# The first mixer's recurrence over blocks of 128 tokens instead of chunks of 64, with a second, further decayed copy of half the queries

## What is computed

```
def _gla_scan(q, k, v, log_a, s0):        # CHUNK = 64
    def step(s, inp):
        qc, kc, vc, gc = inp
        b = jnp.cumsum(gc, axis=2)
        b_last = b[:, :, -1:, :]
        q_dec = qc * jnp.exp(b)
        scores = jnp.einsum('bhld,bhmd->bhlm', q_dec, kc * jnp.exp(-b))
        scores = jnp.where(mask, scores, 0.0)
        o = (jnp.einsum('bhlm,bhmv->bhlv', scores, vc)
             + jnp.einsum('bhld,bhdv->bhlv', q_dec, s))
        s_new = (jnp.exp(b_last[:, :, 0, :, None]) * s
                 + jnp.einsum('bhld,bhlv->bhdv', kc * jnp.exp(b_last - b), vc))
        return s_new, o
```

## Time and profile before

| | us |
|---|---|
| three runs | 2849.07, 2850.6, 2851.8 |
| median | 2850.6 |
| span of the profiled execution | 2836.0 |
| PE busy in that span | 2684.6 (95%) |
| DVE busy | 1397.8 (49%) |
| ACT busy | 1005.6 (35%) |
| the eight GLA scans | 1636 to 1936 |

### The profile page before, as it was taken

How to read it: one execution, slowest core, us unless ns; L and a number is a source line. 1 busy time by engine, 2 the same in 40 slices (tenths; PEclk the granted TensorE clock), 3 DMA queues, 4 the chain that set the end, 5 groups by cost and what they waited for, 6 DMA issues and landing times.

```text
span 2836.0 us, 36376 instructions
## 1 busy us (share of the span) xinstructions
PE 2684.6 (95%) x14292; PEld 2183.0 (77%) x14292; DVE 1397.8 (49%) x1833; ACT 1005.6 (35%) x1694; POOL 818.7 (29%) x645
## 2 busy tenths in 40 slices
PE   7988999999999889999999899998999899999998
PEld 6966788888798667888887676666877688788887
DVE  2748755543327586554433445546445534433332
ACT  5458622222244695222222444353223200222222
POOL 5566623343236465244343010031001011100000
PEclk9999999999999999999999899998999999999999
DMA  6230034554422100355454111111112133233232
GB/s 134 84 62 1 11 88 134 150 140 125 132 85 82 49 1 27 90 141 152 131 141 132 33 49 45 42 33 45 45 32 59 30 104 116 74 93 104 80 92 81
DMA packets 396730, 230.46 MB, mean 81 GB/s; under 512 B 9772, under 2 KB 392876, under 8 KB 396560
## 3 DMA queue, kind: packets, MB, share of 16 engines
q1 hardware_dynamic: 394608, 226.19, 28.7%
q0 software_dynamic: 1952, 1.94, 0.9%
HBM read 226.01 MB, written 2.10 MB: 80 GB/s over the span
## 4 chain that ended last, share of the span: by engine, by line
PE 77%; DVE 9%; ACT 7%; DMA 5%; issue 2%; SPq 0%; POOL 0%; DVEq 0%; ACTq 0%; POOLq 0%
PE ps L842 65%; PE scores L842 8%; DMA raws<-in_w_down 4%; PE ps L987 1%; ACT wH L1841 1%; DVE R L2193 1%; DVE wL L2403 1%; DMA ring<-in_w_in 1%; DVE ring_parts L2456 1%; DVE spare L2203 0%; ACT U L1680 0%; DVE R L2521 0%; DVE QK_parts L2183 0%; ACT spare L1703 0%; ACT R L1708 0%
## 5 line engine op out<-in xcount | busy, mean ns | idle before, releaser
L842 PE MATMUL ps<-xH,wH 128*128 128x512 f32 x1000 | 395.0, 395 | 6.5 <-DVE xL L2378 4.1
L842 PE MATMUL ps<-xL,wH 128*128 128x512 f32 x1000 | 390.7, 391 | 0.0
L842 PE MATMUL ps<-xH,wL 128*128 128x512 f32 x1000 | 390.0, 390 | 0.0
L1841 ACT ACTIVATE wH<-raws 128x2048 fp32r<-128x2048 f32 (+1 forms) x114 | 193.0, 1693 | 495.2 <-PE ps L842 356.6
L842 PE MATMUL ps<-ring_parts,U_parts 128*128 128x256 f32 (+2 forms) x2000 | 337.8, 296 | 18.8 <-DVE ring_parts L2260 6.2
L2403 DVE TENSOR_TENSOR wL<-raws,wH 128x2048 fp32r<-128x2048 f32 (+1 forms) x114 | 231.7, 2032 | 247.3 <-ACT wH L1841 246.0
L842 PEld LDWEIGHTS ps<-ring_parts,U_parts 128*128 128x128 f32 x2000 | 295.3, 201 | 35.1 <-issue 30.4
L842 PE MATMUL ps<-R 128*64 128x128 f32 (+3 forms) x1688 | 242.1, 334 | 30.7 <-DVE R_parts L2214 7.0
L808 POOL CAST ring_parts<-ring 128x2048 fp32r<-128x2048 f32 x34 | 67.0, 1969 | 648.9 <-DMA ring<-in_w_in 573.5
L733 POOL TENSOR_TENSOR spare<-spare,cvec 128x1024 f32<-128x1024 f32 x64 | 122.8, 1919 | 441.3 <-DMA spare<-in_w_ada 441.3
L842 PEld LDWEIGHTS ps<-R 128*64 128x64 f32 (+2 forms) x1688 | 157.3, 166 | 112.1 <-issue 61.8
(11 more groups left out here) (444 smaller groups left out, 4762.5 us busy)
## 6 DMA issues: line engine op xcount, KB each, us to landing
raws<-in_w_gate_up SPq DMA_DIRECT2D x88, 512.0 KB, 5.6
ring<-in_w_in SPq DMA_DIRECT2D x34, 1024.0 KB, 5.7
spare<-in_w_ada SPq DMA_DIRECT2D x64, 512.0 KB, 3.9
raws<-in_w_down SPq DMA_DIRECT2D x32, 704.0 KB, 6.0
raws<-in_w_ffn_in SPq DMA_DIRECT2D x44, 512.0 KB, 5.1
ring<-in_w_in SPq DMA_DIRECT2D x26, 512.0 KB, 5.4
raws<-in_w_ffn_out SPq DMA_DIRECT2D x16, 704.0 KB, 4.6
ring<-in_w_o SPq DMA_DIRECT2D x12, 448.0 KB, 3.7
```

The costliest lines, as they stand in the source:

```text
L842: return nc.tensor.matmul(o, a, b, start=first, stop=last)
L1841: ap.do(f(wH[:, g % 2, 0:n], raws[:, g % 2, 0:n], ACT.Copy), wh_ready)
```

## The change

The GLA recurrence goes over 6 blocks of 128 tokens instead of 12 chunks of 64. The sums of the decay logarithms still run inside 64-token chunks, so the query and key factors stay as they are. What crosses from one chunk of a block to the other is put together from their parts:

- `ends` holds for each chunk what the state decays by up to the block's end; its two small operations stand in `decay_sums` ahead of the subtraction that gives the keys' factor.
- `qd` has three groups of 64 queries for each tile: the first chunk's, the second chunk's, and the second chunk's scaled by the decay through the first. `decayed` makes that copy with one more multiplication, and the decay of a block (`block_decay`) with another small one. The wait for ACT's `dec` moves from ahead of `masked` into `decayed`.
- The scores matmul takes all three groups (192 columns), so four tiles need two banks. `masked` makes two copies for each bank.
- There are 5 state jobs of 128 rows instead of 11 of 64, with six filler matmuls behind each, and 4 DVE steps of the recurrence behind the first copy instead of 10.
- An output job is two matmuls of 128 x 128 weights instead of one such and two of 128 x 64.
- The table `tri` grows from 256 to 384 columns. `ST` and `qd` lie in the memory that `ST` had.

```diff
-                bank = db.fill(pe)
-                for j in range(TT):
-                    ins = mm(bank[:, j * P:(j + 1) * P], ki[:, d, j * P:(j + 1) * P], qd[:, d, j * P:(j + 1) * P], True, True)
-                ins.then_inc(d_full, 1)
+                for pair in range(2):
+                    bank = db.fill(pe)
+                    for n in range(2):
+                        j = 2 * pair + n
+                        ins = mm(bank[:, n * 3 * CH:(n + 1) * 3 * CH], ki[:, d, j * P:(j + 1) * P],
+                                 qd[:, d, j].rearrange("p g c -> p (g c)"), True, True)
+                    ins.then_inc(d_full, 1)
...
-                order = gla_order(d)[:-1]
-                for c in order:
-                    b_, t = c % 2 * CH, c // 2
-                    job(db, lambda b: b[:, 0:DV], [(kdt[b_:b_ + CH, t, :], v_[b_:b_ + CH, t, 0:DV])])
-                    if order.index(c) % 2:
-                        some(beside_states, 2)
+                for t in block_order(d)[:-1]:
+                    job(db, lambda b: b[:, 0:DV], [(kdt[:, t, :], v_[:, t, 0:DV])])
+                    some(beside_states, 2)
...
                 for j in range(TT):
-                    bank = db.fill(pe)
-                    mm(bank[:, 0:DV], SC[:, d, j, :], v_[:, CT + j, 0:DV], True, False)
-                    for half in range(2):
-                        s_ = gla_order(d).index(4 + 2 * j + half)
-                        ins = mm(bank[half * CH:(half + 1) * CH, 0:DV], qd[:, d, j * P + half * CH:j * P + (half + 1) * CH],
-                                 ST[:, s_, 0:DV], False, True)
-                    ins.then_inc(d_full, 1)
+                    s_ = block_order(d).index(CT + j)
+                    job(db, lambda b: b[:, 0:DV], [(SC[:, d, j, :], v_[:, CT + j, 0:DV]),
+                                                   (block_queries(d, j), ST[:, s_, 0:DV])])
...
-                vp.do(v.tensor_tensor(W1.rearrange("p (c l) -> p c l", l=CH), bc(last, CH, 2), b, ALU.subtract), b2_ready)
+                vp.do(v.tensor_copy(ends[:, :], last))
+                vp.do(v.tensor_tensor(ends[:, d::2], last[:, d::2], last[:, 1 - d::2], ALU.add))
+                vp.do(v.tensor_tensor(W1.rearrange("p (c l) -> p c l", l=CH), bc(ends[:, :], CH, 2), b, ALU.subtract), b2_ready)
...
+                vp.more(dec_ready)
+                vp.do(v.tensor_tensor(block_decay[:, d, :], dec[:, d, 0::2], dec[:, d, 1::2], ALU.mult))
+                through = dec[:, d, 4 + d::2]
+                vp.do(v.tensor_tensor(qd[:, d, :, 2 - 2 * d, :], qd[:, d, :, 2 * d, :], bc(through, CH, 2), ALU.mult))
...
             def masked(d):
-                bank = db.take(dve)
-                vp.do(v.copy_predicated(SC[:, d], bc(tri[:, d, :], TT, 1), bank[:, :].rearrange("p (a c) -> p a c", a=TT)), d_free)
+                for pair in range(2):
+                    bank = db.take(dve)
+                    x = bank[:, 0:2 * 3 * CH].rearrange("p (a c) -> p a c", a=2)
+                    into = SC[:, d, 2 * pair:2 * pair + 2, :]
+                    at_, last = (1 - d) * CH, 2 * d * CH
+                    vp.do(v.copy_predicated(into, bc(tri[:, d, 0:P], 2, 1), x[:, :, at_:at_ + P]))
+                    vp.do(v.copy_predicated(into[:, :, (1 - d) * CH:(2 - d) * CH], bc(tri[:, d, P:P + CH], 2, 1), x[:, :, last:last + CH]), d_free)
                 vp.also(sc_ready)
```

More of the change, by code:

```diff
@@ L130, in build @@
         wup = C[0:2 * RANK, 1536:2560].rearrange("p (a b) -> p a b", a=2)
+        ends = sb("ends", [P, NC2])
+        block_decay = sb("block_decay", [P, 2, NC2 // 2])
         rt = sb("rt", [P, TT])
@@ L2538, in _ @@
             for h in range(NH2):
-                vp.more(dec_ready)
                 masked(0)
@@ L2546, in _ @@
                     second_low("v", h + 1)
-                states(gla_order(0), ST, DV, lambda c: dec[:, 0, c:c + 1])
+                states(block_order(0), ST, DV, lambda c: block_decay[:, 0, c:c + 1])
                 decay_sums(h, 1)
@@ L2554, in _ @@
                 gla_outputs(0)
-                vp.more(dec_ready)
                 masked(1)
-                states(gla_order(1), ST, DV, lambda c: dec[:, 1, c:c + 1])
+                states(block_order(1), ST, DV, lambda c: block_decay[:, 1, c:c + 1])
                 if h + 1 < NH2:
@@ L2656, in mlstm_outputs @@
                     y_subtract(KT - 1, KT)
-                states(mlstm_order(d), STm, DV + 1, lambda c: dec[:, d, c:c + 1])
+                states(block_order(d), STm, DV + 1, lambda c: dec[:, d, c:c + 1])
                 for t in range(TT):
```

26 lines of the change are left out of this document (15 added, 11 removed).

## The result

| | before | after |
|---|---|---|
| median of four runs each, us | 2851.2 | 2819.5 |
| lowest and highest | 2849.07, 2853.16 | 2812.45, 2823.27 |
| span of the profiled execution | 2836.0 | 2810.6 |
| GLA stage: first state copy on DVE to the end of the last output | 288.2 | 257.3 |

The ratio is 0.9895, with a 95% interval from 0.9875 to 0.9915. The forecast was 2819.6. The median fell by 31.7 us, where 31 were forecast. The stage in the last row runs from 1647.70 to 1935.85 before and from 1642.41 to 1899.73 after. It is 30.8 us shorter. The span is only 25.4 us shorter: what lies ahead of the stage took 5.3 us less and what lies behind it 10.7 us more, both in unchanged code. The changed kernel was run and profiled a second time, and there the stage took 261.0 us. The later sections come back to both.

A forecast was written before the change was run, and what follows sets the result against it. PE was taken to bound the GLA scans. 22.8 - 1.9 + 11.2 - 2.1 - 0.7 + 1.3 = 30.6, taken as 31 because the last outputs ran at half clock: 2850.6 - 31 = 2819.6 us, range 2811 to 2832.

The forecast's parts named there:

- State jobs: GLA recurrence on PE: 0.43 us a job against 0.82 to 0.84 a pair; 3.2 us a scan, 22.8 in all.
- Outputs: Output jobs on PE: 0.86 us instead of 1.21, so 0.35 for each of 32 jobs, 11.2 us gained.
- Scores: Scores matmuls on PE: 64 more columns cost 0.43 us for four tiles, paid in five scans, -2.1 us.
- Masks: DVE's masked copies: 1.6 us, about 1 more; hidden except in head 3, direction 0, charged -0.7 us.
- The weights' low halves: PE's three direction 1 waits for DVE's weight subtraction: 0.4 us gained each, +1.3, leaving about 0.3 each.
- Head 3, direction 0: No state gain in this scan: PE waits about 3.6 us more for ACT's permuting copies; clock charged -1.9.
- its charge for the clock: Head 3, direction 0: a second PE gap may bring 3.9 us at half clock, -1.9 us, bounds 0 and -3.5.
- The distance of 14.6 us: Gap between the profiled execution's span, 2836.0 us, and the median of runs, 2850.6, kept unchanged in the forecast.
- the shape is not the price: Rival on state and output jobs: a 128-row job costs 0.84 us like a pair; gain 10, 2840 us; chance 0.07.
- concurrency is all: Rival: a pair of state jobs or output halves costs one matmul, nothing more; 2850 us, no change; chance 0.03.
- another engine catching up: Rival: DVE slack, second scores bank, masks and last-head contention cost 3 + 2 + 4; gain 22, 2829 us; chance 0.12.
- The slower one: Rival: PE's clock at 0.50 more often, GLA stretch mean clock 0.87, time 2857 us; chance 0.03.

The follow-up runs named there:

- the shape alone: The kernel before with all 11 state jobs kept but each contracting 128 rows instead of 64; one run took 2847.9 us.
- the count alone: The kernel before with 5 state jobs for each scan, still of 64 rows, and the matching DVE steps left out; one run took 2840.0 us.
- the outputs alone: The kernel before with only the output jobs changed, to two matmuls of 128 x 128 weights instead of three matmuls; 2836.9 us, ratio 0.9971.
- the states alone: The kernel before with only 5 state jobs of 128 rows and 4 recurrence steps; decays, scores and outputs as they were; 2822.0 us, ratio 0.9922.
- Narrow scores: The changed kernel with the scores undone: four matmuls of 128 columns in one bank, one masked copy of 512 elements; one run took 2805.3 us.
- the low half earlier: The changed kernel with the low-half subtraction for the second mixer's first values moved ahead of head 2, direction 1's outputs; 2809.3 us, ratio 0.9874.
- both edits: The changed kernel with that low-half subtraction moved earlier and POOL permuting six feature tiles instead of five; 2808.9 us, ratio 0.9864.
- a second edit: The changed kernel with six feature tiles permuted by POOL and two by ACT, instead of five and three; 2814.7 us, ratio 0.9891.

## Why the prediction was right

**State jobs: right, both sizes.** Forecast was 0.43 us a job and 3.2 a scan. Measured are 0.42 with fillers of 256 columns and 0.45 with 512. The states of head 1, direction 0, took 10.84 us before and take 1714.87 - 1707.59 + 0.43 = 7.71 now, which is 3.1 less. The experiments show the reason too: at a place in the list neither the shape alone nor the count alone gives anything.

**Outputs: right for the job, with a cost behind them that was not charged.** 0.35 us for each of 32 jobs, by the changed kernel and by the outputs alone. But from the last output of head 0 to the transposes of its norm it takes 5.57 us instead of 4.58, and in head 1 5.33 instead of 4.49. DVE's four scalings there now run beside POOL's cast of the next weights, and take 2.60 us instead of 1.60:

```profile
1711.45 1.60 DVE L2521 TENSOR_SCALAR R<-R,rsg 128x256 f32<-128x256 f32 x4
```

```profile
1696.34 1.89 POOL L811 CAST ring_parts<-ring 128x2048 fp32r<-128x2048 f32 x1 [9.38 <-DMA ring<-in_w_in]
1696.95 2.60 DVE L2533 TENSOR_SCALAR R<-R,rsg 128x256 f32<-128x256 f32 x4
1699.66 1.97 PE L1371 MATMUL ps<-ident,R 128*128 128x128 f32 x8 [1.16 <-DVEq L56]
```

The longer waits appear with the outputs alone (1.44 and 0.80 us) and not with the states alone.

**Scores: too low.** 0.43 was charged for a scan, and narrowing them gives 0.58 back. Over the five scans in which they count that is 0.8 us more than the 2.1 of the sum, within the bound.

**Masks: right in size (1.5 us for 1.6), and right in price where it was charged.** Narrow scores give 0.68 us back from head 2's last output to the transposes in head 3, where 0.7 was charged. Against the kernel before it shows as only 0.08 us (8.11 for 8.03), since the subtraction that queues behind the masks took 2.45 us instead of 2.83.

**The weights' low halves: right, a little better.** Before, 0.73 us each. Forecast were 0.3 us each, and measured 0.22. PE's waits for them in the stage:

```profile
PE ps L845 <- DVE ring_parts L2455: 0.4, 2, 0.2
```

**Head 3, direction 0: the mechanism was right, the sum of it by luck.** PE waits 2.92 us for the permuted tokens instead of a forecast 3.6 (3.97 in the second profile of the changed kernel, 3.8 with the states alone). The scan gains 0.65 us in the first profile instead of nothing and loses 3.07 in the second. The stretch at half clock behind the wait, which was charged with 1.9 us, did not come in the first profile; in the second the clock is 0.50 from 1855 to 1861. These are PE's stretches at that wait (us, PE busy, granted clock, DMA share, GB/s), and ahead of them one between head 0 and head 1, for which nothing had been charged:

```profile
1700.00:1704.00 4.00, 4.00 (x17) 0.64 0.02 4
...
1844.00:1848.00 4.00, 1.11 (x8) 1.00 0.00 0
1848.00:1852.00 4.00, 3.96 (x33) 1.00 0.01 2
```

The first row and the longer wait just ahead of it (1.16 us instead of 0.16) are why head 0 to head 1 took 14.21 us instead of 11.90. So a fall of the clock was charged, and one came, but at another place. From head 1 to head 2 it was the other way round: the clock fell there before and not in the first profile after, which is the 0.93 us that this piece got shorter. Nor was the place in the prediction a fixed one: with the low half earlier the clock was 0.50 from 1852 to 1856, right behind a wait of 4.66 us.

**The sum.** By the pieces of the table, the six scans of heads 0 to 2 give 3.44 + 3.30 + 3.30 + 3.92 + 3.89 + 3.95 = 21.8 us, head 3 gives 0.65 and 2.27, and the pieces between give back 3.4 (3 x 0.25 + 2.31 - 0.93 + 0.64 + 0.59 = 3.36). The outputs give 6 x 1.05 in heads 0 to 2 and 1.38 and 1.84 in head 3, 9.5 together. That is all of the stage's 30.8 us, where 31 were forecast. That the first profile comes so near is partly luck: by the second the stage is 27.2 us shorter. The two differ by the clock. An estimate from the granted clock of slices of 2 us: if each slice is shortened by the share that its clock lacks to 1.00, the stage is 279.6 us before and 247.1 and 247.3 in the two profiles after. That is a gain of 32.3 to 32.5, and the forecast without its charge for the clock is 32.5.

**The distance of 14.6 us was a misreading without effect.** The prediction kept 14.6 us between span and median as if it lay around the span. In the run of the changed kernel that was profiled, the time was 2812.45 and the span 2810.6. So only 1.85 us lie around the span. If the same holds before, its profiled execution took about 2838 us, the fastest of its kernel on record (2838.04 to 2858.4 in later sessions). Since the sum was a difference, nothing hung on it.

**Rivals.** That the shape is not the price would have left state jobs of 0.84 and 2840 us, and the new timeline has 0.42 to 0.45. That concurrency is all needed pairs of 0.43, and the earlier trace rows already had 0.82. The third, another engine catching up, came true in parts: 0.15 us for the second bank, the wait in head 3, and 0.8 to 1.0 us in each of heads 1 and 2 for DVE beside POOL. DVE's slack in direction 1 held, by 0.32 us in head 0 and by almost nothing in head 1. The slower one needed a mean clock of 0.87 in the stage; it was 0.96.

## What to carry to other kernels

In this kernel a small matmul between large ones cost more than its columns: going to 64-row jobs and back took 0.4 us each time, whether one or two stood there. Read this from start to start around the small job, and look in the trace for a full-size job among the same neighbours before you believe a gain. When PE's list gets shorter, look for the place where another engine's chain was already level with it: taking 1.96 us from the first of two waits in a row shortened the way past both by only 0.9, and a second edit that gave 1.3 alone gave 3.8 together with it.

## What was not expected of the hardware

**A DVE operation of six columns took 1.75 us.** POOL's cast and DVE's product in the changed kernel, head 0, direction 1:

```profile
1685.06 1.90 POOL L811 CAST ring_parts<-ring 128x2048 fp32r<-128x2048 f32 x1 [25.08 <-DMA ring<-in_w_in]
```

```profile
1685.22 1.75 DVE L2487 TENSOR_TENSOR block_decay<-dec 128x6 f32<-128x6 f32 x1
```

The same product takes 0.17 us elsewhere. Here it starts 0.16 us behind POOL's cast and ends with it, at 1686.97 and 1686.96. The other way round, one of POOL's copies of the permuted tokens took 2.99 us and the next 1.05. A DVE subtraction had begun ahead of it:

```profile
1827.70 2.99 POOL L633 COPY R<-ring_parts 128x512 f32<-128x512 f32 x1
...
1831.43 1.05 POOL L633 COPY R<-U_parts 128x512 f32<-128x512 f32 x1
```

```profile
1827.32 2.45 DVE L2455 TENSOR_TENSOR ring_parts<-ring,ring_parts 128x2048 fp32r<-128x2048 f32 x1
```

"GPSIMD Engine Reference" of the Trainium skill says in its specifications that POOL shares its SBUF interfaces with DVE, and that they contend where DVE has two SBUF inputs. Both places agree with it: each DVE operation has two inputs in SBUF, and the one that came later went on only when the other had ended or nearly so. The first stall is not new with the change. In the same scan before, a product of DVE that takes 0.69 us elsewhere took 2.43 beside the same cast, so the prediction's 1.02 us of slack had it in already:

```profile
1697.77 2.43 DVE L2482 TENSOR_TENSOR R<-R 128x512 f32<-128x512 f32 x1
```

**Unchanged code is not equally long.** From the last output of the first mixer to the end of the span it took 900.2 us before, 910.9 in the first profile of the changed kernel, 903.8 in the second, and 900.8 to 910.9 in the others, without an edit there. So nothing here says that the change makes the second mixer slower. The clock goes with part of it. The 315 us from 1915 in the first profile of the changed kernel had a mean clock of 0.90, and those from 1945 before 0.93. The spread of whole runs is as large (2800.05 to 2821.13 with both edits). So a gain of a few microseconds is to be read from pieces of a timeline in which the clock stays at 1.00, and a run alone cannot show it. What sets where the clock falls stays open.
